# Expert mixing in half-width column tiles: each gather brings two experts for 64 tokens, and ScalarE writes 128x64 stacked diagonals into the spent half of the buffer

## What is computed

```python
h = h + hybrid_mixer(h, ...)          # RMSNorm, one projection, stick-breaking attention (8 heads),
                                      # sliding-window attention with sinks, output projection
h = h[:, N_META:]
h = h + peer_ffn(rmsnorm(h, ln_ffn), peer_query, peer_sub_keys, expert_u, expert_v)
return rmsnorm(h, final_norm)
```

```python
q = (tb @ w_query).reshape(128, 8, 2, 64)              # 8 heads, two halves
s = einsum('thpd,hpnd->thpn', q, sub_keys)             # 128 keys on each side
s1, i1 = top_k(s[:, :, 0], 16); s2, i2 = top_k(s[:, :, 1], 16)
top_s, pos = top_k(all sums s1 + s2, 16)               # 16 of 256 candidates
idx = take(i1 * 128 + i2, pos)                         # 8 x 16 = 128 experts of 16384 per token
g = softmax(top_s)
act = gelu(einsum('thkd,td->thk', expert_u[idx], tb))
out = einsum('thk,thkd->td', g * act, expert_v[idx])
```

## Time and profile before

| | |
|---|---|
| median of three runs | 3259.25 us (3256.38 to 3265.2) |
| the profiled execution | 3258.49 us |
| its span, first to last instruction | 3256.7 us |
| mean granted clock of TensorE | 0.974 of full speed |
| busy: TensorE, VectorE, ScalarE, GpSimd | 88%, 62%, 46%, 40% |
| HBM | 350 GB/s over the span; 1073.8 of 1143.4 MB are the gathers |
| first gather issued, first product of blocks 0 and 1 | 387.8, 395.6 and 772.1 us |

### The profile page before, as it was taken

How to read it: one execution, slowest core, us unless ns; L and a number is a source line. 1 busy time by engine, 2 the same in 40 slices (tenths; PEclk the granted TensorE clock), 3 DMA queues, 4 the chain that set the end, 5 groups by cost and what they waited for, 6 DMA issues and landing times.

```text
span 3256.7 us, 30483 instructions
## 1 busy us (share of the span) xinstructions
PE 2854.3 (88%) x8606; PEld 1364.6 (42%) x8606; DVE 2020.6 (62%) x4738; ACT 1496.7 (46%) x3712; POOL 1310.1 (40%) x1134
## 2 busy tenths in 40 slices
PE   8999779998998979988899979998897789787776
PEld 5668634433453334433453334433353335332222
DVE  2111685795559754786559755795559755975444
ACT  3051163685437743665438843685332343233222
POOL 1000134444344444444445544445343544345553
PEclk9999899999999999999999999999998999999999
DMA  3541399999999999989999999989999999999998
GB/s 113 176 128 49 136 365 388 398 329 378 385 420 347 347 418 375 401 328 386 393 419 343 347 405 389 396 322 382 379 420 372 412 403 401 402 394 422 421 422 335
DMA packets 200229, 1143.39 MB, mean 351 GB/s; under 512 B 23584, under 2 KB 59760, under 8 KB 68736
## 3 DMA queue, kind: packets, MB, share of 16 engines
q0 software_dynamic: 147456, 1073.81, 82.5%
q1 hardware_dynamic: 52608, 67.67, 6.3%
HBM read 1126.31 MB, written 15.07 MB: 350 GB/s over the span
## 4 chain that ended last, share of the span: by engine, by line
PE 42%; DVE 23%; DMA 21%; issue 8%; ACT 4%; POOL 3%; SPq 0%; POOLq 0%; DVEq 0%; ACTq 0%
PE ps L1468 20%; DMA r_uv<-in_experts,r_wk 20%; DVE r_uv L1155 9%; PE ps L1246 5%; PE ps L1422 4%; PE ps L1405 3%; POOL r_uv L614 3%; PE ps L1207 2%; DVE r_wk L1088 2%; DVE r_wk L994 1%; DVE r_wk L997 1%; DVE r_wk L1003 1%; DVE r_wk L1086 1%; DVE r_wk L1089 1%; PE ps L1276 1%
## 5 line engine op out<-in xcount | busy, mean ns | idle before, releaser
L1468 PE MATMUL ps<-r_uv,r_wk 128*128 128x512 f32 x4096 | 1953.7, 621 | 333.3 <-ACT r_wk L844 323.7
L614 POOL DMA_INDIRECT r_uv<-in_experts,r_wk x1024 | 1202.7, 1175 | 1663.8 <-PE ps L1468 1342.0
L1468 PEld LDWEIGHTS ps<-r_uv,r_wk 128*128 128x128 f32 x4096 | 761.9, 196 | 1350.0 <-issue 853.8
L1155 DVE CUSTOM_DVE_ANT_0 r_uv<-r_uv,hncur 128x1024 f32<-128x1024 f32 x512 | 627.8, 1239 | 429.9 <-DMA r_uv<-in_experts,r_wk 427.6
L1155 DVE CUSTOM_DVE_ANT_0 r_uv<-r_uv,r_wk 128x1024 f32<-128x1024 f32 x512 | 627.0, 1244 | 343.5 <-DMA r_uv<-in_experts,r_wk 335.8
L834 ACT ACTIVATE r_wk<-r_wk 128x2 f32<-128x2 f32 x512 | 104.1, 203 | 1344.5 <-DVE r_wk L1155 1338.7
L844 ACT ACTIVATE r_wk<-cst,r_wk 128x128 f32<-128x128 f32 x1024 | 355.2, 394 | 64.2 <-PE ps L1468 48.2
L840 ACT ACTIVATE r_wk<-r_wk 128x1 f32<-128x1 f32 x1024 | 245.9, 287 | 16.8
L834 ACT ACT_TABLE_LOAD x151 | 193.7, 1283 | 2.7
L637 ACT ACT_TABLE_LOAD x147 | 188.6, 1283 | 6.5 <-PE ps L1398 1.8
L1422 PEld LDWEIGHTS ps<-r_wk,r_wq 128*128 128x128 f32 x1024 | 123.8, 192 | 27.0 <-issue 26.8
(11 more groups left out here) (156 smaller groups left out, 2100.1 us busy)
## 6 DMA issues: line engine op xcount, KB each, us to landing
r_uv<-in_experts,r_wk POOLq DMA_INDIRECT x1024
r_wk<-lkv_dram SPq DMA_DIRECT2D x72, 128.0 KB
r_uv<-in_x SPq DMA_DIRECT2D x8, 512.0 KB, 3.3
hncur<-in_w_chunks SPq DMA_DIRECT2D x8, 512.0 KB, 3.8
h2cur<-in_w_chunks SPq DMA_DIRECT2D x8, 512.0 KB, 3.7
fnb<-in_w_chunks SPq DMA_DIRECT2D x8, 512.0 KB, 3.8
r_wo<-in_w_out SPq DMA_DIRECT2D x8, 512.0 KB, 5.0
r_wk<-in_x SPq DMA_DIRECT2D x8, 512.0 KB
```

Source lines behind the costliest of these rows:

```text
L614: g.indirect_dma_start(uv[:, k % NB, :], None, experts, bass.IndirectOffsetOnAxis(idx[b % 2][:, k:k + 1], 0)).then_inc(rows_in[k % NB], 16)
L1155: v.tensor_tensor_reduce(uv[:, k % NB, 0:D], uv[:, k % NB, 0:D], hn[b % 2][:, :], 1.0, 0.0, ALU.mult, ALU.add, actv[:, k:k + 1]).then_inc( ...
L1468: last = t_.matmul(ps[:, i, :], diag[:, k % 4, :], uv[:, k % NB, D + 512 * i:D + 512 * i + 512], start=k == 0, stop=k == K - 1)
```

## The change

A gather k now serves 64 tokens with two experts each. Partition 64j + s of gather k = 2m + q holds token 64q + s and its expert 2m + j. Two gathers together still bring what two brought before, and there are as many, of the same size. For this, indices and gates are rearranged by `spread` (four small VectorE copies in place of one copy or none), and the tokens that VectorE multiplies with are laid out for both kinds of gather in `hnrep` (two copies of 1024 words a partition, made by four VectorE copies of 64x1024, `repeat_rows`, at the start of each block). ScalarE scales a stacked pair of 64x64 identities, 128x64, and writes it into the first 64 words of the gather's own buffer, whose product is spent; `diag`, its four places and the wait for them are gone. TensorE contracts over all 128 partitions into 64 of the output's partitions: even gathers into partitions 0 to 63, odd ones into 64 to 127. `gel` falls away, the streamed weights use `hnrep` and `h2cur`, two of the staging places lie in `fnb`, and VectorE waits for the last projection before the first `repeat_rows`.

```diff
+HALF = P // GRP
@@
+        ident64 = cst[:, C_ID64:C_ID64 + HALF]
@@
-        hncur = sb("hncur", D)
+        hnrep_v = sb("hnrep", GRP * D)
+        hnrep = grid(hnrep_v[:, :], GRP)
         h2cur = sb("h2cur", D)
-        wchunk = [grid(view[:, :], DC) for view in (hncur, h2cur, fnb)]
+        wchunk = [grid(view, DC) for view in (hnrep[:, 0, :], hnrep[:, 1, :], h2cur[:, :])]
@@
-        stage = [view[:, GW * u:GW * u + GW] for view in (lw1_v, diag_v) for u in range(2)]
+        stage = [view[:, GW * u:GW * u + GW] for view in (lw1_v, fnb) for u in range(2)]
@@
                 for n in range(NG):
                     act.wait_ge(dotted, K * b + GRP * (n + 1))
-                    link(a.activation(gel[:, GRP * n:GRP * n + GRP], actv[:, GRP * n:GRP * n + GRP], ACT.Gelu))
+                    link(a.activation(actv[:, GRP * n:GRP * n + GRP], actv[:, GRP * n:GRP * n + GRP], ACT.Gelu))
...
-                    act.wait_ge(rows_used, K * b + GRP * n + GRP - 4 + NB)
                     for k in range(GRP * n, GRP * n + GRP):
-                        a.activation(diag[:, k % 4, :], ident, ACT.Copy, scale=gel[:, k:k + 1]).then_inc(diag_ready, 1)
+                        a.activation(uv[:, k % NB, 0:HALF], ident64, ACT.Copy, scale=actv[:, k:k + 1]
+                                     ).then_inc(diag_ready, 1)
@@
+            def spread(into, of, n0, n1):
+                for q in range(GRP):
+                    for j in range(GRP):
+                        last = v.tensor_copy(
+                            into[HALF * q:HALF * q + HALF, n0:n1].rearrange("p (m j) -> p m j", j=GRP)[:, :, j],
+                            of[HALF * j:HALF * j + HALF, n0:n1].rearrange("p (m q) -> p m q", q=GRP)[:, :, q])
+                return last
+
+            def repeat_rows():
+                for q in range(GRP):
+                    for j in range(GRP):
+                        last = v.tensor_copy(hnrep[HALF * q:HALF * q + HALF, j, :], hnn[HALF * j:HALF * j + HALF, :])
+                link(last)
@@
-                    v.tensor_copy(idx[t % 2], idxf).then_inc(idx_ready, 1)
+                    spread(idx[t % 2], idxf, 0, K).then_inc(idx_ready, 1)
@@
-                    v.tensor_tensor(gn3, gn3, gsum.unsqueeze(2).to_broadcast([P, PH, TOPK]), ALU.mult
-                                    ).then_inc(routed, 1)
+                    link(v.tensor_tensor(gn3, gn3, gsum.unsqueeze(2).to_broadcast([P, PH, TOPK]), ALU.mult))
+                    spread(gates[t % 2], gn, 0, K).then_inc(routed, 1)
@@
-                v.tensor_copy(idx[0][:, TOPK * h:TOPK * h + TOPK], idxf3[:, h, :]).then_inc(head_ready, 1)
+                spread(idx[0], idxf, TOPK * h, TOPK * h + TOPK).then_inc(head_ready, 1)
@@
-                v.tensor_scalar(gate_h, gate_h, gsum[:, h:h + 1], None, ALU.mult).then_inc(gates_ready, 1)
+                link(v.tensor_scalar(gate_h, gate_h, gsum[:, h:h + 1], None, ALU.mult))
+                spread(gates[0], gn, TOPK * h, TOPK * h + TOPK).then_inc(gates_ready, 1)
@@
             head_gates(0)
+            dve.wait_ge(proj_summed, NP)
@@
                 first = b == 0
+                if b:
+                    dve.wait_ge(dotted, K * b)
+                repeat_rows()
@@
-                            v.tensor_tensor_reduce(uv[:, k % NB, 0:D], uv[:, k % NB, 0:D], hn[b % 2][:, :], 1.0, 0.0,
+                            v.tensor_tensor_reduce(uv[:, k % NB, 0:D], uv[:, k % NB, 0:D], hnrep[:, k % GRP, :], 1.0, 0.0,
@@
-                            last = t_.matmul(ps[:, i, :], diag[:, k % 4, :],
-                                             uv[:, k % NB, D + 512 * i:D + 512 * i + 512], start=k == 0,
-                                             stop=k == K - 1)
+                            last = t_.matmul(ps[HALF * (k % GRP):HALF * (k % GRP) + HALF, i, :], uv[:, k % NB, 0:HALF],
+                                             uv[:, k % NB, D + 512 * i:D + 512 * i + 512], start=k < GRP,
+                                             stop=k >= K - GRP)
```

More of the change, by code:

```diff
@@ L149 @@
 C_LNM = C_GAIN + 8
-C_ALL = C_LNM + DC
+C_ID64 = C_LNM + DC
+C_ALL = C_ID64 + HALF
 class Own:
@@ L241, in block_program @@
         small = sb("small", 64)
[L242 to L246, removed]
+        r_wk = sb("r_wk", 12320)
+        (pT_v, ssb_v, sq_v, qT_v, hs, hnn, in_v, topv_v, topf_v, cs_v, ci_v,
+         lw1_v, tops_v, posf_v, idxf, idx1, g1, actv, gn, idx0, g0) = parts(r_wk, [
+             2048, 2048, D, D, D, D, 512 + P + 512, 256, 256, PH * NC, PH * NC,
+             512, K, K, K, K, K, K, K, K, K])
         TOP_AT = 2 * 2048 + 4 * D + 512 + P + 512
@@ L263, in block_program @@
         topv, topf = grid(topv_v, 16), grid(topf_v, 16)
-        topi = grid(topi_v.bitcast(U32), 16)
+        topi = grid(topf_v.bitcast(U32), 16)
         cs, ci = grid(cs_v, PH), grid(ci_v, PH)
         tops, posf = grid(tops_v, PH), grid(posf_v, PH)
-        pos = grid(pos_v.bitcast(U32), PH)
-        gates, gates3 = (g0, g1), (grid(g0, PH), grid(g1, PH))
+        pos = grid(posf_v.bitcast(U32), PH)
+        gates, gn3 = (g0, g1), grid(gn, PH)
         idxf3 = grid(idxf, PH)
         idx = (idx0.bitcast(U32), idx1.bitcast(U32))
-        hn = (hnn, hncur)
-        diag = grid(diag_v, 4)
         lq_v, *lkv = parts(in_v, [512] + [2 * P] * 2)
@@ L648, in front @@
                 act.wait_ge(x_in[u], 16 * m + 16)
-                link(a.activation((hncur, h2cur)[u][0:rows, :], xt[0:rows, u, :], ACT.Square,
+                link(a.activation((hnrep[:, 0, :], h2cur)[u][0:rows, :], xt[0:rows, u, :], ACT.Square,
                                   accum_out=nssq[0:rows, u:u + 1]))
@@ L839, in experts_of @@
                     for k in range(GRP * n, GRP * n + GRP):
-                        last = a.activation(gel[:, k:k + 1], gel[:, k:k + 1], ACT.Copy, scale=gates[b % 2][:, k:k + 1])
+                        last = a.activation(actv[:, k:k + 1], actv[:, k:k + 1], ACT.Copy, scale=gates[b % 2][:, k:k + 1])
                     link(last)
-                    act.wait_ge(rows_used, K * b + GRP * n + GRP - 4 + NB)
                     for k in range(GRP * n, GRP * n + GRP):
-                        a.activation(diag[:, k % 4, :], ident, ACT.Copy, scale=gel[:, k:k + 1]).then_inc(diag_ready, 1)
+                        a.activation(uv[:, k % NB, 0:HALF], ident64, ACT.Copy, scale=actv[:, k:k + 1]
+                                     ).then_inc(diag_ready, 1)
                     if n == 1 and b:
@@ L1045, in tile_step @@
                     polish(r3[:, 1:2], r3[:, 0:1], D)
-                    v.scalar_tensor_tensor(out=hn[t % 2][:, :], in0=hs, scalar=r3[:, 1:2], in1=lnb[:, :],
+                    v.scalar_tensor_tensor(out=hnn, in0=hs, scalar=r3[:, 1:2], in1=lnb[:, :],
                                            op0=ALU.mult, op1=ALU.mult).then_inc(hn_ready, 1)
@@ L1500, in constants @@
     c[:, C_IOTA:C_IOTA + NC] = np.arange(NC)
+    c[:, C_ID64:C_ID64 + HALF] = s % HALF == np.arange(HALF)[None, :]
     part = np.concatenate([[0] * META, [1] * CHUNK, [2] * CHUNK, [3] * CHUNK])[None, :]
```

15 lines of the change are left out of this document (7 added, 8 removed).

## The result

The changed kernel takes 3237.7 us (median of 6 runs, 3226.8 to 3244.0), the kernel before in the same comparison 3258.8 (6 runs, 3250.4 to 3268.6): a ratio of 0.9929, 95% interval 0.9905 to 0.9953. It is faster by 0.7%, 21 us, where the prediction had 70. The time lies in its range, the direction is right, and the size is a third of what was said. The profiled execution took 3238.06 us.

What follows compares the result with a forecast made beforehand. It took transfers to bound block 7 and the query stretch, TensorE alone groups 14 to 23, with three engines nearly full late. 3258.5 - 52 - 38 - 4 + 3 + 6 + 14 = 3187.5, said as 3188 us; range 3145 to 3268.

Steps and rivals of the forecast that it cites:

- the first rival: All gathers: the halves don't run side by side, all three gains vanish and VectorE's copies stay, 3268 us; chance 8%.
- Two column tiles run together: TensorE's gather pairs: both halves run side by side, 1.71 us for a group's two gathers in place of 3.43.
- Late stretch, -38: Groups 34 to 63: a third of TensorE's 113 us relief shortens the path, -38 us, bounds nothing and -107.
- Mix stretch, -52 and +14 for the clock: Groups 14 to 23, seven blocks: shorter groups save 52 us, entering at 1.2 GHz costs 14.
- Query stretch, -4: Query groups, seven blocks: group and step fall from 5.37 to 3.65 us, 352.1 goes to 347.9, -4 us.
- spread, +6: Block 0's heads: extra small index and gate copies, every 0.09 us, cost VectorE 6 us, bounds 0 and 7.
- repeat_rows, +3: Block starts: four copies, 2.75 us a block, mostly hidden, cost 3 us over seven blocks, bounds 0 and 19.
- Block 7 at the floor: Block 7: already at the transfers' pace, 2.485 us a gather, so nothing changes.
- Halves in series: All gathers: the second gather starts only when the first is done, 3268 us; chance 8%.
- Strict order: Gather pairs: the second's first record starts only with the first's last, pair 3.0 us, total 3234 us; chance 7%.
- The third rival: Late stretch: TensorE's more than thought, all of the 107 us come, 3119 us; chance 8%.
- The clock rival: Groups 14 to 31: the clock stays low in mix and query, 3312 us at half of it; chance 9%.

Runs made afterwards that it cites:

- the halves in turn: The changed kernel with TensorE waiting before each odd gather until the even one is done: 3292.1 us, ratio 1.0114.
- the second profile: The changed kernel run once more, unchanged, on the chip of the follow-up runs, against the kernel before: 3240.3 us, ratio 0.9943.

## Why the prediction was right or wrong

The sign was right and so was the mechanism of the mix stretch, the overlap of the halves. The path of the late stretch was wrong, and with it the size, 70 us forecast and 21 measured. The measured 3237.7 lies outside the forecast's own range (3150 to 3235) and inside the wide one only because its upper end was set for the first rival. By the prediction's own steps:

- **Two column tiles run together: right.** The pair takes 1.87 us from start to start instead of 1.71 (mix timeline, 867.57 to 869.44), and 2.17 from the first start to the last end, in place of 3.70, where the odd diagonal comes 0.24 us later. Shown by the halves in turn (1.0114).
- **Late stretch, -38: the step that failed.** The prediction read VectorE's 97 us at 92 busy in block 5 and still gave a third of TensorE's relief to the path. Measured together with `repeat_rows` (+3): -6.3 (-1.3 by the second profile), a miss of 29. Taking another 102 us from TensorE in five windows brought nothing, and doubling 40.8 us of VectorE's work cost 37.5 us in the changed kernel and 38.3 in the one before: those groups were VectorE's already, at TensorE busy 92 to 99%. Of the prediction's bounds the one marked nothing, VectorE ends last anyway, was close to the truth.
- **Mix stretch, -52 and +14 for the clock: -23.8 instead of -38.** Two sizes. The clock: the groups are entered at 1.2 GHz as forecast, but that costs 20.8 us (383.6 less 362.8) and not 14. The delay is smaller than the 5.2 us a block of the forecast, 3.3 in block 1 (the squares 1.7, the pair 1.5; `mix` is at the full clock again), but nearly all of it stays, 3.0 a block, where 2 had been counted. The change of tile width: 1.87 + 3.63 = 5.50 us a group where the sum had 1.71 + 3.43 + 0.1 = 5.25; times 28 groups that is 7 us, the rest of the miss. The trace of before had bounded it at under 0.2 us for both changes; here the two cost 0.36.
- **Query stretch, -4: +1.1**, within what two executions differ by. It stood at the transfers' floor already, 50.3 us a block against 49.7, so at most those 0.6 us a block were there to win.
- **spread, +6: +10.2**, shown by the run without it (82.0 against 93.0). The count was right, the price was not: the row of 0.09 us was of other shapes, and these come every 0.18 to 0.22. The Trainium skill (VectorE: DVE Perf Modes, Two Vector instructions with no wait between them) says that a VectorE instruction which starts on another group of 32 partitions than the one ahead, in its input or its output, starts only when that one has finished. The copies of `spread` change between partitions 0 and 64 each time; the two of the earlier trace rows stay where they are, and the second starts 0.09 us after a first of 0.17. The trace agrees with the rule, since the four index copies shown above last 0.17 us each and together 0.71, one after another, but no run here changed the partitions alone.
- **repeat_rows, +3**: 2.5 to 7.6 by the run without it, right within what such a run tells, and far from the bound of 19.
- **Block 7 at the floor: right**, 2.485 us a gather, at a clock of 0.83. The mean clock of 0.87 lies in the range named.
- **The rivals.** Halves in series and strict order fell with the overlap. Strict order is worth a word: the Trainium skill (TensorE: Matmul & The Clock Gate, Part 3) has matmuls start and end in program order; here four records of the odd gather, which stand behind the even one's four, run beside them, so the measurement decides against the rule for matmuls in different columns. That rival's time, 3234, is the nearest to the measured one, by chance; by its own price of 6.43 us a mix group it would save 19 us in the ten groups and not 24, which makes it 3239. The third rival's place was the right one to doubt, in the other direction. The clock rival had its mechanism at the entry of the mix stretch, not through it and not in the query stretch, where the granted clock is 0.93 to 1.00 (groups 24 to 33).

Sum of the misses: 29 (late) + 14 (mix) + 5 (query) + 4 (spread) = 52, less 2 for the stages ahead and block 7, of the 50.5 us between 3187.5 and 3238.06.

Of the marks that were set: VectorE's 7.2 us wait for `mix_done` became 3.1, not nothing.

```profile
884.19 1.28 DVE L1057 SCALAR_TENSOR_TENSOR r_wk<-ps,small,r_wk 128x1024 f32<-128x1024 f32 x1 [3.12 <-PE ps L1427]
```

Groups 14 to 23 take 53.2 to 56.6 us and not 50 to 53, and the late windows 180 to 187 and not 172 to 180. VectorE is busy 155 of the 184 us of block 1's late window. Of the idle rest, 29 us, its waits are 17 us for rows and 9 for ScalarE, and 20 us of it lie outside groups 41 to 57. What stays open is which of these waits a better order could save.

## What to carry to other kernels

Where two engines are nearly full in the same window, take nothing for a relief of one before the other is ruled out, and ask by doubling: work added to VectorE in the kernel before cost 94% of itself in windows where TensorE stood at 92 to 99% busy. Halving TensorE's time in stretches where it isn't the bound lowers its clock, and the bill comes in the next dense stretch; a few matmuls of no use ahead of it gave back 14 to 19 us, but in the kernel before, where they made a backlog, the same ones cost 46. Small copies have a fixed price; count them by the row of the same shape and partitions, here 0.2 us each.

## What was not expected of the hardware

- Matmuls into different column halves, each behind a semaphore of its own, overlap though queued one behind the other: the pair takes 2.17 us from first start to last end where full width takes 3.70. A wait of the second half for the first costs more than the lost overlap: 7.55 us for a group, against 6.86 in the kernel before.
- Each change between half and full width costs about 0.2 us (`mix` 3.63 instead of 3.43, the pair 1.87 instead of 1.71).
- TensorE can leave a stretch of waiting at half its clock and pay for it in the next one: 3.57 us for the sums of squares and 3.48 for a pair behind an idle 3.38 us, in place of 1.84 and 1.94.
- With TensorE busy 58% instead of 74% in block 7 the granted clock is 0.83 instead of 1.00, at the same pace of the gathers.
- Copies of 1024 words on 64 partitions take as long as on 128: 2.79 us for four, 0.70 each, beside 0.687.
